# Four split buffers, four open sums in the mix and output products, and a wide value pair in a fused decoder layer on one core

## The chip, the cores and the metric

The kernel runs on one core of one Trainium2 chip. Time is device time in microseconds (us) for one execution of the whole program, the median of several executions.

## What is computed

One decoder layer on 256 tokens of width 1024, in float32, with weights read from HBM. The reference, cut to what matters:

```python
h = x
u = rms_norm(h, norm_mix)
z = u @ w_in                                  # 1024 x 3328
y_rwkv = rwkv7_time_mix(z[:, :1792], ...)     # 8 heads of 64, a recurrence over 256 steps
q, k, v = split(z[:, 1792:], 3)               # 8 heads of 64
y_moba = moba_attention(q, k, v)              # one block of 256: plain causal attention
h = h + concat([y_rwkv, y_moba]) @ w_mix_out
h = h + cross_attention(rms_norm(h, norm_xattn), rms_norm(mem, norm_mem), w_xq, w_xkv, w_xo)  # 4 heads of 256
a = square(relu(rms_norm(h, norm_ffn) @ w_ff1))    # 1024 x 4096
h = h + a @ w_ff2                                  # 4096 x 1024
out = rms_norm(h, norm_final)
```

## The kernel before

**Dense products.** All weights are cut into 65 units of 1 MB (UNITS): z is the part of the input projection for the recurrence, mq and mv the queries, keys and values of the first attention, xk and xv those of the cross-attention's memory, xq its queries, mix and xo the two output products, f1 and f2 the feed-forward part. A unit is loaded by SP into one of three raw buffers and worked off in two halves s. Every half is split for accuracy: ScalarE's hi(s) copies it to w_hi in the rounded type fp32r, VectorE's lo(s) writes the rest, raw - w_hi, to w_lo. TensorE then makes three products for each k: high x high, high x low, low x high. A buffer of w_hi and w_lo is one of NSPLIT = 3, taken in turn, so hi(s) waits for dense_mm, which counts the finished halves, to reach s - 2.

**Quarters.** A half is done in two quarters; QUARTERS lists them as (half, part), 260 in all, and dense(n) in TensorE's program issues the next n. In most units a quarter is 4 of the 8 k steps (12 matmuls of 256 columns). For mix and xo units 0 and 1 the list mixes the quarters of four halves, so that those parts come first whose input is ready first: in mix the attention's part 1, in xo the first two heads' part 0. Sums lie in two banks, dense_bank[0] and [1] (bank 6 and 7), and take(o) on VectorE takes the finished sum o away. A unit is wide (wide_of) if it holds 512 columns of 4 k steps instead of 256 columns of 8; then two units make a pair, the tokens are the stationary side and a matmul is 512 columns long (lines 488 to 490). Only xv 0 and 1 are wide before; mv 0 and 1 use lines 502 to 504, with 256 columns.

**The small work between them.** TensorE's program is a hand-written list in which small steps stand between the calls of dense: mats, right, join and solve (the inverse of the recurrence's blocks), outq, phi, psi, state, states_out (the recurrence over 8 chunks), pair_scores, pair_flip, pair_values (first attention, two heads at a time), scores, turn, values (cross-attention, a head at a time), deviation, normalize, gate (end of the recurrent part). ScalarE and VectorE have lists of their own with the same names, in which hi, lo and take stand between the small steps. blocks() is VectorE's step that inverts 16 x 16 blocks by rank-one updates, one after another; join(0, .) needs its first result, join(1, .) its second and a copy by ScalarE. For head h of the cross-attention scores(h) goes to VectorE (scale, maximum), ScalarE (exponential), VectorE (weigh), TensorE (turn, a transpose), ScalarE (copy), TensorE (values), and then two copies split the result for xo. Every engine works strictly in the order of its list and waits at semaphores.

Of the kernel before, what the change touches and what calls it, by code (L numbers as in the profile page):

```python
# [18 lines left out]
NRAW, NSPLIT = 3, 3  # L19
# [12 lines left out]
def units():  # L32
# [5 lines left out]
    out += [("mv", "w_in", 0, base + 2 * RW + 256 * j, j) for j in range(2)]  # L38
# [18 lines left out]
def wide_of(u):  # L57

    what, _, _, _, j = UNITS[u]
    return  what == "xv" and j < 2  # L60
# [56 lines left out]
def build(nc, io, out):  # L117
# [3 lines left out]
    with ctx:  # L121
# [6 lines left out]
        def flat(x):  # L128
            return x.rearrange("p a t -> p (a t)")
# [30 lines left out]
        btok = sb("btok", [128, NT, RW])  # L160
# [154 lines left out]
        def half_bank(s):  # L315
            return dense_bank[(s + 1) % 2]

# [128 lines left out]
        def _(pe):  # L446
# [4 lines left out]
            def quarter(q):  # L451
# [73 lines left out]
                dst = b[:, (s % 2) * T:(s % 2) * T + T]  # L525
# [434 lines left out]
            spread(0)  # L960
            dense(8)
            lora()
            spread(1)
            dense(4)
            key_sums()
            load(1, 0)
            dense(3)
            keys(0)
            load(1, 1)
            dense(15)  # L970
            tokens()
            dense(2)
            bonus()
            dense(1)
            vtokens()
            dense(3)
# [4 lines left out]
            dense(2)  # L981
            mats(1, 0)
            mats(1, 1)
            load(1, 2)
            mats(1, 2)
            mats(1, 3)
            dense(3)
            right(0)
            right(1)
            dense(2)  # L990
            load(1, 3)
            dense(1)
            join(0, 0)
            join(0, 1)
            join(1, 0)
            dense(2)
            join(1, 1)
            dense(2)
            pair_scores(0)
            solve(0)  # L1000
# [3 lines left out]
            dense(2)  # L1004
            outq(0, 0)
            pair_flip(0)
            dense(2)
            pair_values(0)
            outq(0, 1)
            outq(0, 2)  # L1010
            pair_scores(1)
            outq(0, 3)
            dense(5)
            pair_flip(1)
            outq(1, 0)
# [3 lines left out]
            dense(3)  # L1019
# [3 lines left out]
            dense(3)  # L1023
            pair_scores(2)
            psi(0, 0)
# [7 lines left out]
            dense(3)  # L1033
            state(1)
            pair_flip(2)
            state(2)
            dense(1)
            pair_values(2)
            state(3)
            dense(1)  # L1040
            state(4)
            dense(1)
            state(5)
            pair_scores(3)
            state(6)
            dense(1)
# [4 lines left out]
            dense(1)  # L1051
            normalize()
            dense(3)
            pair_values(3)
            gate()
            dense(20)
# [6 lines left out]
            dense(3)  # L1063
# [6 lines left out]
            dense(1)  # L1070
# [4 lines left out]
            turn(3)  # L1075
            values(3)
            dense(40)
            rms(3)
            dense(47)
            residual(0)  # L1080
            dense(2)
            residual(1)
            dense(34)
            residual(2)
            dense(14)
            residual(3)
            dense(6)
# [3 lines left out]
        def _(act):  # L1091
# [24 lines left out]
            def follow(o):  # L1116
                what, j = OUTS[o][3:5]
                if what == "z":

                    act.wait_ge(dve_params, 2)  # L1120
                    act.wait_ge(out_taken, o + 1)
                    for a in range(2):
                        t = 2 * j + a
                        last = op(zT[:, t, :], tmp[:, 0, a * T:a * T + T], ACT.Copy, scale=onemu[:, t:t + 1])
                    last.then_inc(act_rest, 1)
# [15 lines left out]
            def part(n, half):  # L1141
# [5 lines left out]
                op(tmp[:, n % 2, T * half:T * half + T], half_bank(s)[:, T:2 * T], ACT.Copy).then_inc(act_part, 1)  # L1147
# [204 lines left out]
            hi(3)  # L1352
            follow(0)
            hi(4)
            stats(1)
            hi(5)
            follow(1)
            hi(6)
            gates()
            hi(7)  # L1360
            hi(8)
            follow(2)
            rates()
            key_sums()
            hi(9)
            key_norm()
            follow(3)
            hi(10)
            hi(11)
            decays()  # L1370
            hi(12)
            follow(4)
            hi(13)
            factor()
            load(1, 0)
            hi(14)
            hi(15)
            load(1, 1)
            follow(5)
            hi(16)  # L1380
            follow(6)
            hi(17)
            hi(18)
            tokens()
            hi(19)
            vtokens()
            hi(20)
            hi(21)
            hi(22)
            hi(23)  # L1390
            right(0)
            right(1)
            hi(24)
            load(1, 2)
            join()
            hi(25)
            hi(26)
            right(2)
            load(1, 3)
            right(3)  # L1400
            solve(0)
            hi(27)
            pair_scores(0)
            hi(28)
            solve(1)
            hi(29)
            pair_flip(0)
            pair_values(0)
            hi(30)
            pair_scores(1)  # L1410
            hi(31)
            outq(0)
            hi(32)
            hi(33)
            pair_flip(1)
            outq(1)
            pair_values(1)
            hi(34)
            pair_scores(2)
            hi(35)  # L1420
            source_out(0)
            source_out(1)
            source_out(2)
            hi(36)
            pair_flip(2)
            pair_values(2)
            source_out(3)
            hi(37)
            pair_scores(3)
            hi(38)  # L1430
            deviation()
            hi(39)
            deviation_root()
            pair_flip(3)
            hi(40)
            hi(41)
            hi(42)
            pair_values(3)
            gate(0)
            gate(1)  # L1440
            hi(43)
# [5 lines left out]
            hi(49)  # L1447
            operand("mix", 0)
            operand("mix", 1)
            operand("mix", 2)  # L1450
            hi(50)
            operand("mix", 3)
            hi(51)
            hi(52)
            rms(2)
            hi(53)
            hi(54)
            scores(0)
            hi(55)
            turn(0)  # L1460
            hi(56)
            hi(57)
            scores(1)
            values(0)
            hi(58)
            turn(1)
            scores(2)
            hi(59)
            values(1)
            hi(60)  # L1470
            turn(2)
# [920 lines left out]
```

## Time and profile before

| | |
|---|---|
| median of 3 executions | 467.77 us (467.44 to 468.75) |
| the profiled execution | 468.22 us, span 465.9 us |
| matmuls (PE) busy | 453.1 us, 4488 instructions |
| VectorE (DVE) busy | 320.4 us |
| ScalarE (ACT) busy | 233.8 us |
| granted TensorE clock, mean | 0.997 of 2.4 GHz |

The span runs from the first to the last instruction. Of TensorE's busy time one should know that matmuls overlap in the profile: one is drawn from its start to a modelled end, and the next starts long before that end. What a matmul costs the engine is the distance from its start to the next one's. In the trace's rows a time in brackets is the engine's idle time just before an instruction, with the engine and line that ended it.

### The profile page before, as it was taken

The page shows a single profiled execution, that of the slowest core. Times are in us where ns is not written, and L with a number is a line of the kernel's source. Part 1 is how long each engine was busy: PE and PEld are TensorE (multiplying, and loading weights), DVE is VectorE, ACT ScalarE, POOL GpSimd, SP SyncE. Part 2 cuts the span into 40 slices and gives each one's busy share as a digit, 9 for nine tenths or more (in the row PEclk, how much of TensorE's full clock was granted, in tenths as well). Part 3 has the DMA queues.
Part 4 walks back from the last instruction along what each step waited for, and adds up shares of the span by engine and source line. Part 5 has one row for each costly group of instructions (what it writes and reads, how often), then busy time and mean ns, then how long its engine had stood idle before and what let it go on. Part 6 is the DMA issues. An engine that isn't in the chain of part 4 may idle for free.

```text
span 465.9 us, 10518 instructions
## 1 busy us (share of the span) xinstructions
PE 453.1 (97%) x4488; PEld 410.9 (88%) x4488; DVE 320.4 (69%) x487; ACT 233.8 (50%) x373; POOL 35.1 (8%) x51
## 2 busy tenths in 40 slices
PE   7999999899999999999998999999999999999994
PEld 7999999889998789999997998888888888888883
DVE  4878997887667579579665476846575648555675
ACT  5897843044442544436544355545453544455444
POOL 8200000000000000062000001250000000000000
PEclk9999999999999999999999999999999999999998
DMA  8955544602343223554343256565656474865502
GB/s 258 344 165 174 171 133 138 184 4 94 117 164 112 91 93 110 162 182 166 113 140 126 78 156 218 179 192 174 188 186 204 145 250 141 281 183 184 181 0 90
DMA packets 60385, 73.05 MB, mean 157 GB/s; under 512 B 1314, under 2 KB 49524, under 8 KB 60340
## 3 DMA queue, kind: packets, MB, share of 16 engines
q1 hardware_dynamic: 60260, 72.14, 48.3%
q8 instruction: 35, 0.57, 0.5%
q0 software_dynamic: 80, 0.26, 0.2%
q14 instruction: 10, 0.08, 0.1%
HBM read 71.35 MB, written 1.05 MB: 155 GB/s over the span
## 4 chain that ended last, share of the span: by engine, by line
PE 95%; ACT 2%; DVE 1%; issue 1%; DMA 1%; SPq 0%
PE bank L534 13%; PE bank L549 11%; PE bank L550 11%; PE bank L551 11%; PE bank L568 6%; PE bank L566 6%; PE bank L567 6%; PE bank L536 6%; PE bank L502 2%; PE bank L503 2%; PE bank L504 2%; PE bank L946 2%; PE bank L922 2%; PE bank L488 1%; PE bank L616 1%; PE bank L533 1%
## 5 line engine op out<-in xcount | busy, mean ns | idle before, releaser
L1622 DVE TENSOR_TENSOR w_lo<-raw,w_hi 128x1024 fp32r<-128x1024 f32 x130 | 159.7, 1237 | 55.8 <-ACT w_hi L1114 55.4
L1114 ACT ACTIVATE w_hi<-raw 128x1024 fp32r<-128x1024 f32 x130 | 136.9, 1057 | 101.8 <-PE bank L568 41.7
L534 PE MATMUL bank<-op,w_hi 128*128 128x512 f32 x256 | 89.7, 399 | 0.0
L549 PE MATMUL bank<-op,w_hi 128*128 128x256 f32 x288 | 83.5, 290 | 0.7 <-DVE w_lo L1622 0.7
L551 PE MATMUL bank<-op,w_lo 128*128 128x256 f32 x288 | 81.5, 283 | 0.0
L550 PE MATMUL bank<-op,w_hi 128*128 128x256 f32 x288 | 81.4, 283 | 0.0
L536 PE MATMUL bank<-op,w_lo 128*128 128x256 f32 x224 | 62.9, 281 | 0.0
L549 PEld LDWEIGHTS bank<-op,w_hi 128*128 128x128 f32 x288 | 55.2, 192 | 1.5 <-ACT w_hi L1114 0.8
L550 PEld LDWEIGHTS bank<-op,w_hi 128*128 128x128 f32 x288 | 55.2, 192 | 0.2
L551 PEld LDWEIGHTS bank<-op,w_lo 128*128 128x128 f32 x288 | 55.2, 192 | 0.0
L534 PEld LDWEIGHTS bank<-op,w_hi 128*128 128x128 f32 x256 | 46.6, 188 | 8.9
L566 PE MATMUL bank<-w_hi,op_hi 128*128 128x512 f32 x128 | 50.0, 390 | 0.0
L568 PE MATMUL bank<-w_hi,op_lo 128*128 128x512 f32 x128 | 49.8, 389 | 0.0
L567 PE MATMUL bank<-w_lo,op_hi 128*128 128x512 f32 x128 | 49.8, 389 | 0.0
L536 PEld LDWEIGHTS bank<-op,w_lo 128*128 128x128 f32 x224 | 42.3, 189 | 1.2
L549 PE MATMUL bank<-op_hi,w_hi 128*128 128x256 f32 x128 | 37.2, 290 | 0.0
L550 PE MATMUL bank<-op_lo,w_hi 128*128 128x256 f32 x128 | 36.2, 283 | 0.0
L551 PE MATMUL bank<-op_hi,w_lo 128*128 128x256 f32 x128 | 36.2, 283 | 0.0
L1702 DVE TENSOR_TENSOR tmp<-bank,tmp 128x256 f32<-128x256 f32 x32 | 13.3, 421 | 24.7 <-ACT tmp L1147 24.4
L567 PEld LDWEIGHTS bank<-w_lo,op_hi 128*128 128x128 f32 x128 | 24.0, 188 | 5.0
L568 PEld LDWEIGHTS bank<-w_hi,op_lo 128*128 128x128 f32 x128 | 24.0, 188 | 5.0
L566 PEld LDWEIGHTS bank<-w_hi,op_hi 128*128 128x128 f32 x128 | 24.0, 188 | 4.7
(277 smaller groups left out, 713.4 us busy)
## 6 DMA issues: line engine op xcount, KB each, us to landing
raw<-in_w_ff SPq DMA_DIRECT2D x32, 1024.0 KB, 5.3
raw<-in_w_in SPq DMA_DIRECT2D x12, 1024.0 KB, 6.1
raw<-in_w_xkv SPq DMA_DIRECT2D x8, 1024.0 KB, 5.4
raw<-in_w_mix_out SPq DMA_DIRECT2D x4, 1024.0 KB, 5.1
raw<-in_w_xq SPq DMA_DIRECT2D x4, 1024.0 KB, 5.8
raw<-in_w_xo SPq DMA_DIRECT2D x4, 1024.0 KB, 5.1
xval<-in_x SPq DMA_DIRECT2D x2, 512.0 KB, 4.9
raw<-in_w_in SPq DMA_DIRECT2D x2, 512.0 KB, 5.8
```

Source lines behind the costliest of these rows:

```text
L502: mm(dst, hi, wh[:, k, :], start=(xk == 0), stop=False)
L534: last = mm(b[:, :], wh[:, k, :], op_both[0][:, :, k, :], start=first, stop=final)
L536: mm(b[:, 0:T], wl[:, k, :], op_hi[0][:, k, :], start=False, stop=False)
L549: mm(dst, wh[:, k, :], op_hi[which][:, k, :], start=first, stop=False)
L550: mm(dst, wh[:, k, :], op_lo[which][:, k, :], start=False, stop=False)
L551: last = mm(dst, wl[:, k, :], op_hi[which][:, k, :], start=False, stop=final)
L566: mm(dst[:, :], hi, wh[:, k, :], start=first, stop=False)
L567: mm(dst[:, :], hi, wl[:, k, :], start=False, stop=False)
L568: last = mm(dst[:, :], lo, wh[:, k, :], start=False, stop=final)
L1114: op(view(w_hi), r, ACT.Copy).then_inc(hi_done, 1)
L1622: tt(view(w_lo), r, view(w_hi).bitcast(f32), ALU.subtract).then_inc(lo_done, 1)
L1702: tt(x, half_bank(s)[:, 0:T], x, ALU.add).then_inc(dve_add, 1)
```

## The change

- NSPLIT goes from 3 to 4: a fourth buffer of w_hi and w_lo.
- Room for it: tmp keeps one buffer of its own, its second is the first half of mval, free by then; btok moves into xval.
- mv 0 and 1 become a wide pair: 4 k steps of 512 columns each, with the loads (4 x 512 instead of 8 x 256), the matmuls and the takes of a pair.
- In mix and xo units 0 and 1 the second halves' sums get columns 0 to 255 of bank 1 and bank 2 (second_bank). So four sums can be open, and QUARTERS takes all four early parts first, then the four late ones. TensorE waits for dve_norm before the first such half of mix, and take adds the two halves with two operations.
- The lists of TensorE, ScalarE and VectorE are reordered throughout.

```diff
-NRAW, NSPLIT = 3, 3
+NRAW, NSPLIT = 3, 4
...
-    out += [("mv", "w_in", 0, base + 2 * RW + 256 * j, j) for j in range(2)]
+    out += [("mv", "w_in", 4 * j, base + 2 * RW, j) for j in range(2)]
...
-    return  what == "xv" and j < 2
+    return what == "mv" or what == "xv" and j < 2
...
         QUARTERS += [(2 * _u + _i, _late ^ _p ^ 1) for _i, _p in
-                     ((0, 0), (2, 0), (0, 1), (1, 0), (1, 1), (2, 1), (3, 0), (3, 1))]
+                     ((0, 0), (1, 0), (2, 0), (3, 0), (0, 1), (1, 1), (2, 1), (3, 1))]
...
-        tmp = sb("tmp", [128, 2, 512])
+        tmp = [sb("tmp", [128, 512])[:, :], mval[:, 0, :]]
...
-        btok = sb("btok", [128, NT, RW])
+        btok = flat(xval).rearrange("p (h n c) -> p h n c", h=2, n=NT)[:, 0, :, :]
...
+        def second_bank(o):
+
+            what, j = OUTS[o][3:5]
+            return B[1 + j][:, 0:T] if what in ("mix", "xo") and j < 2 else dense_bank[o % 2][:, T:2 * T]
...
-                dst = b[:, (s % 2) * T:(s % 2) * T + T]
+                dst = second_bank(o) if s % 2 else b[:, 0:T]
+                if what == "mix" and s % 2 and q == BEGUN[s]:
+                    pe.wait_ge(dve_norm, 1)
...
+                    if j < 2:
+                        for a, x in enumerate((dense_bank[o % 2][:, 0:T], second_bank(o))):
+                            last = tt(h[:, a, :], x, h[:, a, :], ALU.add)
+                        last.then_inc(out_taken, 1)
+                        return
...
             join(0, 0)
             join(0, 1)
+            load(1, 2)
+            load(1, 3)
+            dense(6)
             join(1, 0)
-            dense(2)
             join(1, 1)
-            dense(2)
             pair_scores(0)
```

TensorE at the first join, where neu,X is join(0, 0) and (0, 1), neu alone join(1, 0), and xkey the transposes of load. Before:

```order
L504 MATMUL bank7<-w_hi,op0 128x256
L756 MATMUL bank0<-neu,X 32x32 x64
L756 MATMUL bank1<-neu 32x32 x32
L502 MATMUL bank6<-w_hi,op0 128x256
L503 MATMUL bank6<-w_lo,op0 128x256
```

and of the change:

```order
L495 MATMUL bank7<-w_hi,op0 128x512
L763 MATMUL bank0<-neu,X 32x32 x64
L623 MATMUL bank4<-ident,xkey 128x128 x4
L623 MATMUL bank5<-ident,xkey 128x128 x4
L493 MATMUL bank6<-w_hi,op0 128x512
```

The two loads now stand behind join(0, .), and join(1, .) follows six quarters later. The list ahead of it, from mats(1, 3) on, is dense(4), right(0), right(1), dense(1) now, and was dense(3), right(0), right(1), dense(2), load(1, 3), dense(1).

VectorE at the end of blocks(), whose last instruction is the transpose. Before:

```order
L1894 STREAM_TRANSPOSE neu<-neu 128x16x2x16
L1622 TENSOR_TENSOR w_lo<-raw,w_hi 128x1024
L1676 TENSOR_TENSOR mqk<-bank6,rinv 128x512
L1622 TENSOR_TENSOR w_lo<-raw,w_hi 128x1024
L1740 SCALAR_TENSOR_TENSOR op1_lo<-bank4,par,op1_hi 128x256 x2
```

and of the change:

```order
L1903 STREAM_TRANSPOSE neu<-neu 128x16x2x16
L1685 TENSOR_TENSOR mqk<-bank6,rinv 128x512
L1626 TENSOR_TENSOR w_lo<-raw,w_hi 128x1024 x4
L1926 TENSOR_SCALAR s2<-s2,par 128x256 x4
L1749 SCALAR_TENSOR_TENSOR op1_lo<-bank4,par,op1_hi 128x256 x2
```

take(10), the row that writes mqk, comes directly behind blocks(); the splits of four halves follow it in one run, and bonus_bias (s2) has moved here.

TensorE at the end of the cross-attention, where probT,xval is values and ident,prob is turn. Before, values(2), turn(3) and values(3) with nothing between:

```order
L551 MATMUL bank7<-op1_hi,w_lo 128x256
L946 MATMUL bank4<-probT,xval 128x256 x4
L934 MATMUL bank5<-ident,prob 128x128 x4
L946 MATMUL bank4<-probT,xval 128x256 x4
L549 MATMUL bank6<-op1_hi,w_hi 128x256
```

and of the change:

```order
L558 MATMUL bank1<-op1_hi,w_lo 128x256
L953 MATMUL bank4<-probT,xval 128x256 x4
L941 MATMUL bank5<-ident,prob 128x128 x4
L556 MATMUL bank6<-op1_hi,w_hi 128x256
L557 MATMUL bank6<-op1_lo,w_hi 128x256
...
L558 MATMUL bank6<-op1_hi,w_lo 128x256
L953 MATMUL bank4<-probT,xval 128x256 x4
L556 MATMUL bank2<-op1_hi,w_hi 128x256
```

A quarter of xo stands between turn(3) and values(3); the sums in bank 1 and bank 2 are the second halves.

## Rows read from the trace of the kernel before

**Rows 1.** The page's first part: matmuls, busy us, share, instructions.
```profile
PE 453.1 (97%) x4488; PEld 410.9 (88%) x4488; DVE 320.4 (69%) x487; ACT 233.8 (50%) x373; POOL 35.1 (8%) x51
```

**Rows 2.** The page's costliest groups: line, engine, operation | busy, mean ns | idle before, releaser.
```profile
L1114 ACT ACTIVATE w_hi<-raw 128x1024 fp32r<-128x1024 f32 x130 | 136.9, 1057 | 101.8 <-PE bank L568 41.7
```

**Rows 3.** The waits of TensorE: line <- awaited: us in total, times, longest.
```profile
PE bank L737 <- issue: 1.3, 1, 1.3
PE bank L946 <- DVE op_lo L2020: 1.0, 1, 1.0
PE bank L756 <- ACT neu L1254: 0.8, 1, 0.8
PE bank L549 <- DVE w_lo L1622: 0.7, 1, 0.7
```

**Rows 4.** TensorE in order of time (start, length), dense, small, dense again.
```profile
116.11 0.28 PE L549 MATMUL bank<-op_hi,w_hi 128*128 128x256 f32 x1
...
118.14 0.28 PE L551 MATMUL bank<-op_hi,w_lo 128*128 128x256 f32 x1
118.35 0.34 PE L798 MATMUL bank<-X,zT 32*64 32x32 f32 x16
...
119.64 0.36 PE L549 MATMUL bank<-op_hi,w_hi 128*128 128x256 f32 x1
119.84 0.28 PE L550 MATMUL bank<-op_lo,w_hi 128*128 128x256 f32 x1
```

**Rows 5.** The same view, first and last of 48 matmuls of the down projection.
```profile
302.27 0.40 PE L566 MATMUL bank<-w_hi,op_hi 128*128 128x512 f32 x1
...
312.93 0.39 PE L568 MATMUL bank<-w_hi,op_lo 128*128 128x512 f32 x1
```

**Rows 6.** The same view from the last mats to the first join.
```profile
87.69 0.74 PE L737 MATMUL bank<-AR,s 64*32 64x64 f32 x50 [1.33 <-issue]
88.36 0.38 PE L549 MATMUL bank<-op,w_hi 128*128 128x256 f32 x1
...
99.18 0.60 PE L616 MATMUL bank<-ident,xkey 128*128 128x128 f32 x4
...
101.15 1.03 PE L756 MATMUL bank<-neu,X 32*32 32x32 f32 x93
```

**Rows 7.** VectorE in order of time: blocks(), its first row and its two results.
```profile
90.19 1.12 DVE L1878 STREAM_TRANSPOSE neu<-neu 128x512 f32<-128x512 f32 x1
...
99.39 1.14 DVE L1890 STREAM_TRANSPOSE neu<-neu 128x512 f32<-128x512 f32 x1
...
100.94 1.08 DVE L1894 STREAM_TRANSPOSE neu<-neu 128x512 f32<-128x512 f32 x1
```

**Rows 8.** TensorE in the cross-attention: turn L934, scores L922, values L946, dense L549.
```profile
230.40 0.60 PE L934 MATMUL bank<-ident,prob 128*128 128x128 f32 x4
...
232.38 0.47 PE L549 MATMUL bank<-op,w_hi 128*128 128x256 f32 x1
...
236.88 1.89 PE L946 MATMUL bank<-probT,xval 128*128 128x256 f32 x8
238.42 0.47 PE L549 MATMUL bank<-op,w_hi 128*128 128x256 f32 x1
...
248.23 0.60 PE L934 MATMUL bank<-ident,prob 128*128 128x128 f32 x4
...
250.82 0.47 PE L549 MATMUL bank<-op_hi,w_hi 128*128 128x256 f32 x1
...
257.91 0.47 PE L549 MATMUL bank<-op_hi,w_hi 128*128 128x256 f32 x1
```

**Rows 9.** VectorE for the last head: scale, maximum, weigh.
```profile
251.21 0.69 DVE L2006 TENSOR_SCALAR prob<-bank 128x512 f32<-128x512 f32 x1 [0.96 <-PE bank L922]
251.94 0.69 DVE L2007 TENSOR_REDUCE small<-prob 128x2 f32<-128x512 f32 x1
...
253.98 0.62 DVE L2014 TENSOR_SCALAR prob<-prob,small 128x256 f32<-128x256 f32 x2
```

More of the change, by code:

```diff
@@ L960, in _ @@
             spread(0)
+            dense(6)
+            lora()
             dense(8)
-            lora()
+            key_sums()
             spread(1)
-            dense(4)
-            key_sums()
+            dense(2)
+            keys(0)
+            dense(14)
             load(1, 0)
[L967 to L970, printed above, removed]
             tokens()
@@ L973, in _ @@
             bonus()
+            vtokens()
             dense(1)
-            vtokens()
-            dense(3)
             mats(0, 0)
@@ L1003, in _ @@
             solve(3)
-            dense(2)
+            dense(3)
             outq(0, 0)
+            outq(0, 1)
+            outq(0, 2)
             pair_flip(0)
@@ L1018, in _ @@
             outq(1, 3)
-            dense(3)
+            dense(2)
             pair_values(1)
@@ L1023, in _ @@
             dense(3)
+            psi(0, 0)
             pair_scores(2)
-            psi(0, 0)
+            dense(2)
             psi(0, 1)
@@ L1032, in _ @@
             psi(1, 3)
-            dense(3)
+            dense(1)
             state(1)
+            dense(2)
+            state(2)
             pair_flip(2)
-            state(2)
+            state(3)
             dense(1)
             pair_values(2)
-            state(3)
-            dense(1)
             state(4)
@@ L1043, in _ @@
             state(5)
+            dense(1)
+            state(6)
             pair_scores(3)
-            state(6)
-            dense(1)
             states_out()
@@ L1062, in _ @@
             scores(1)
-            dense(3)
+            dense(2)
             values(0)
@@ L1069, in _ @@
             values(1)
-            dense(1)
+            dense(2)
             turn(2)
@@ L1499, in _ @@
             hi(74)
+            part(2, 0)
+            hi(75)
             part(2, 1)
+            part(3, 0)
             follow(34)
-            hi(75)
             hi(76)
-            part(3, 0)
             hi(77)
+            follow(35)
             part(3, 1)
@@ L1682, in shift @@
                     t = 2 * j + a
-                    last = stt(out=zT[:, t, 1:T], in0=tmp[:, 0, a * T:a * T + T - 1], scalar=gain("rwkv_mu", t),
+                    last = stt(out=zT[:, t, 1:T], in0=tmp[0][:, a * T:a * T + T - 1], scalar=gain("rwkv_mu", t),
                                in1=zT[:, t, 1:T], op0=ALU.mult, op1=ALU.add)
@@ L1700, in add @@
                 dve.wait_ge(act_part, 2 * n + half + 1)
-                x = tmp[:, n % 2, T * half:T * half + T]
+                x = tmp[n % 2][:, T * half:T * half + T]
                 tt(x, half_bank(s)[:, 0:T], x, ALU.add).then_inc(dve_add, 1)
@@ L2049, in _ @@
             load(0, 1)
-            copies(0)
             load(0, 2)
@@ L2054, in _ @@
             params(1)
+            copies(0)
             diagonal_of(0)
@@ L2059, in _ @@
             lo(3)
+            lo(4)
+            sides()
             follow(0)
-            lo(4)
+            lo(5)
+            take(1)
             copies(1)
-            take(1)
-            lo(5)
-            lo(6)
             diagonal_of(1)
             follow(1)
+            lo(6)
+            lo(7)
+            lo(8)
             take(2)
             follow(2)
-            lo(7)
-            lo(8)
+            lo(9)
+            sums()
+            take(3)
+            lo(10)
+            lo(11)
+            key_norm()
+            follow(3)
             spread_copy(1)
-            sums()
-            key_norm()
-            take(3)
             key_root()
-            lo(9)
-            lo(10)
-            follow(3)
-            lo(11)
+            lo(12)
+            take(4)
             keys(0)
-            take(4)
             keys(1)
-            lo(12)
+            lo(13)
             follow(4)
-            lo(13)
             take(5)
+            lo(14)
             keys(2)
-            lo(14)
-            keys(3)
             lo(15)
@@ L2214, in _ @@
             values(0)
-            lo(57)
+            scores(2)
             lo(58)
-            scores(2)
+            lo(59)
             weigh(2)
```

406 lines of the change are left out of this document (200 added, 206 removed).

## The prediction, made before the changed kernel was run

> **What bounds the kernel now.** The page's first part comes first: matmuls occupy TensorE for 97% of a 465.9 us span [rows 1]. The profiled execution took 468.22 us, 2.3 us more than its span; the median of the three runs is 467.77 us, so a sum made against the profile is lowered by 0.45 us at the end. A busy share can hide small gaps, because a 256-column matmul is drawn 0.28 us long while the next one starts after 0.12 us [rows 4]. So I read starts, not lengths. In the long stretches the starts are evenly spaced, and the list of TensorE's waits holds only a few microseconds [rows 3]. TensorE sets the time, and there are only three ways to shorten it: fewer columns or cheaper instructions on it, fewer changes between dense and small work, and the few waits. Idle time of the other engines is worth nothing by itself. The copies that split the weights (w_hi, ScalarE) follow 101.8 us of idling, mostly for TensorE itself [rows 2]: they are early. No wait in the list is for a buffer that has not been freed. A fourth split buffer alone therefore brings nothing; it only permits the new orders.
>
> **The attention's value units as a wide pair.** Before, they are 96 matmuls of 256 columns: two units, two halves, two parts, four k, three products. The start of one follows that of the last by 0.119 us: 17 steps from 116.11 to 118.14 [rows 4]. After, they are 48 of 512 columns. The down projection has the same form, and there 47 steps take from 302.27 to 312.93, 0.227 us each [rows 5]. 96 x 0.1194 = 11.46 us become 48 x 0.2268 = 10.89 us, a gain of **0.57 us**, all on TensorE's path. At least nothing is lost (the columns are the same), so 0 to 0.6.
> The trace shows 0.119 and 0.227 us, so each instruction carries some 12 ns beside its columns. The Trainium skill (TensorE: Matmul & The Clock Gate, Back-to-back issue gap) gives an isolated gap of N/2.4 + 2.5 ns; as an estimate from that page the pair would gain only 0.1 us. The same section gives 131 ns as the sustained spacing at 512 columns, by which it would gain 5 us; the rows speak against both.
>
> **Fewer changes of work.** A small block between dense quarters costs extra at both ends: 118.14 to 118.35 going out, 119.64 to 119.84 coming in [rows 4], each 0.08 to 0.09 us above the step, 0.17 us together. The order has 41 separate dense stretches before and 38 after: 3 x 0.17 = **0.5 us** (0 to 0.6).
>
> **The end of the cross-attention.** From turn(2) at 248.23 to the dense stretch at 257.91 pass 9.68 us [rows 8]. The work in it, by the undisturbed rows of the same group: turn with scores 1.98 (230.40 to 232.38), a quarter with its changes 12 x 0.119 + 0.17 = 1.60, values 1.54 (236.88 to 238.42) twice, turn 1.98 - 1.54 = 0.44; together 7.10. So 2.58 us are waits, of which the list names 1.0 for op_lo [rows 3]; most of the rest hides in drawn lengths. The cause is that turn(3) and values(3) stand directly behind values(2), while VectorE and ScalarE still make the softmax. After, xo's second halves have banks of their own, so two quarters more can be opened: xo's first quarter moves ahead of turn(2), which lets take(28) be ready for scores(3), one quarter stands between turn(3) and values(3), another behind values(3). Counted from turn(2) = 0: scores(3) ends at 1.98, the quarter at 3.58. VectorE's scaling starts 0.4 after the scores end (250.82 [rows 8] to 251.21) and with the maximum ends 1.42 later, at 252.63 [rows 9]; so values(2) can start at 3.87, a wait of 0.3. Exponential and weighing take from 252.63 to 254.60 [rows 9], 1.97, so turn(3) starts at 5.85 against 5.41, a wait of 0.45. Values(3) comes 1.6 us after turn(3)'s end, and what it needs is two copies of 0.6: no wait. 2.58 becomes 0.75: **1.8 us** gained. If a copy or split that stands between them on ScalarE or VectorE is late, 1 us less; if the order hides all, 2.6.
>
> **The wait of join(1, 0).** Before, it follows join(0, 1) at once and waits 0.8 us for ScalarE's copy [rows 3]. After, two loads and six quarters lie between. **0.8 us** go.
>
> **What is late instead.** The inverse's blocks() are a chain on VectorE. The last mats ends at 88.36 [rows 6]; blocks() begins at 90.19, its first result is there at 99.39 + 1.14 = 100.53, 12.2 us after the mats, and its second at 102.02, 13.7 us after [rows 7]. Before, TensorE came to join(0, 0) at 101.15, 12.8 us after the mats [rows 6], in time, having done six quarters, both right() and a load. After, it has five quarters, one of them wide, and no load: 12.8 - 1.43 - 0.5 (the load with its change) - 0.07 = 10.8 us. It waits 1.4 us. Just behind it the second part of the wide unit needs the bank that take(10) frees, and take(10) is queued behind all of blocks(): 13.7 + 0.6 + 0.1 = 14.4. TensorE, after that wait, arrives there at 12.2 + 1.4 (two join; 93 of their 128 instructions are drawn 1.03 us long [rows 6]) + 0.7 (two loads) = 14.3. So the two waits fall together, **1.5 us lost** in all. Queued behind them on VectorE is lo(23), ready at 15.5, wanted at 15.9. If VectorE is 0.4 us later, that adds; if blocks() starts earlier, at most 0.5 is won back: loss 1.0 to 2.3.
>
> **The issue gap in mats.** TensorE stood 1.33 us in mats(1, 2), waiting for no other engine [rows 3, 6]. It had then issued some 230 matmuls since mats(0, 0) in 6 us. After, the same count is reached about 1 us later, but mats(1, 0) to (1, 3) stand in one piece. The trace of before cannot tell whether it stays whole (0) or goes (1.33). I take the middle, **0.7 us**.
>
> **At no cost, with the cover named.** The first wait, 0.7 us for w_lo [rows 3], stays, since the split that ends it keeps its place behind ScalarE's squares of x, which the change does not touch. take of mix and xo 0 and 1 becomes two VectorE operations of 256 columns, about 0.1 us more each: the next user of the bank comes two quarters (2.9 us) later. mix's four open sums give the gate chain four quarters of cover instead of two: the two quarters more, 2.9 us, cover what the earlier place of gate() takes away. btok inside xval and tmp inside mval need no new wait of TensorE: xval is next written by take(17), behind state(6). The Pool sums and all weight DMAs keep their order; the value pair's two DMAs carry the same megabyte each in longer rows. The DMA of unit u still waits for both splits of unit u - 3, which come no later.
>
> **Sum.** 0.57 + 0.5 + 1.8 + 0.8 - 1.5 + 0.7 = 2.9 us. 468.2 - 2.9 = 465.3 for an execution like the profiled one, 464.9 against the median; I say **465.0 us**.
>
> **Rivals.**
> *The waits only move.* In a fixed order each engine stands where its next instruction stands. If the cross-attention keeps 1.5 us more than I count, because of a split queued ahead of the softmax, and the issue gap stays (0.7), 2.2 of the 2.9 are gone: 467.0. For it: my walk leaves values(2) and turn(3) with no slack at all. Against: both waits are short there, and the covers added are whole quarters.
> *More is won.* The issue gap goes (0.6 beyond the sum) and VectorE reaches blocks() 0.5 earlier: 463.9.
> *Slower: ScalarE and VectorE stand in line for the fourth buffer.* With four buffers a split may run further ahead and is placed so, but its turn comes before the half that frees it is done, and what stands behind it is held. The place: source_out(2) behind hi(38), the state steps behind both; then lo(43) ahead of gate_lo, and in the feed-forward part() behind hi(). Its price is up to one quarter, 1.43 us, each time. It decides once four such places fall on the path: 5.7 - 2.9 gives 470.6. Against: the idling before w_hi is 101.8 us over 130 copies, so a held copy has room, and the state steps keep a dense quarter between most of them.
> *The change does nothing for the path* except the columns: 467.2, if new waits eat the rest; it joins the first rival.
>
> **How the numbers follow.** A measurement of this kernel can tell about 0.3%, 1.4 us, from no change. The forecast with its unknowns (464.2 to 466.3) has 0.50; more is won 0.18; the waits only move (466.4 to 467.9) 0.23; slower by the queue 0.09. Faster by over 0.3% (under 466.4) is 0.50 + 0.18 + a little of the moved waits = 0.70, within 0.3% 0.22, slower 0.08. The ends of my unknown costs are: pair 0 to 0.6, changes 0 to 0.6, cross-attention 0.8 to 2.6, late blocks -2.3 to -1.0, issue gap 0 to 1.33. The range 463.4 to 467.3 leaves out the tails where several of them fall on the same side.
>
> **What would show it.** In the profile after: 48 matmuls of 128x512 in the value units, 0.227 us apart; no wait of join(1, 0) but one of 1.3 to 1.5 us at join(0, 0), for VectorE's blocks; from turn(2) to the dense stretch behind values(3) about 1.8 us less waiting; the issue wait absent or smaller; the feed-forward stretch unchanged in its steps. I am wrong if TensorE waits in the state steps, ahead of gate_lo, or in the feed-forward part, or if join(0, 0) does not wait.

## The result, and the profile after

The changed kernel takes **474.27 us** (median of 5 runs, 473.71 to 474.55); the kernel before, run beside it, 467.91 us (5 runs, 467.44 to 468.79). The ratio is 1.0133, 95% interval 1.0119 to 1.0146: slower by 1.3%, where 465.0 us (463.4 to 467.3) was predicted. The profiled execution has a span of 472.2 us against 465.9.

The page's first part, to set beside [rows 1], shows that hardly anything was added to any engine's work:
```profile
PE 452.8 (96%) x4440; PEld 407.8 (86%) x4440; DVE 320.4 (68%) x489; ACT 234.0 (50%) x373; POOL 35.5 (8%) x51
```
48 matmuls are gone, as planned. (The splits' idle time is 98.4 us against the 101.8 of [rows 2].) The loss must be idle time or a lower clock of TensorE. Its waits (line <- awaited: us in total, times, longest), to set beside [rows 3]:
```profile
PE bank L744 <- issue: 2.2, 1, 2.2
PE bank L558 <- issue: 2.2, 1, 2.2
PE bank L763 <- DVE neu L1899: 1.5, 1, 1.5
PE bank L763 <- issue: 1.3, 1, 1.3
PE bank L623 <- DMA xval<-in_x: 1.1, 1, 1.1
PE bank L606 <- DMA prob<-in_rwkv_ln_b: 1.0, 1, 1.0
PE bank L556 <- DVE op L1702: 0.9, 1, 0.9
```
The reader should see three things. Where [rows 3] had one "issue" of 1.3 us, there are three, together 5.7. There is one wait for blocks() (L763, neu), 1.5, and no wait for ScalarE's neu. And there is a wait of 0.9 for an operand (L1702) that nobody had foreseen. "issue" means that the engine waited for nothing that the profile shows, for no semaphore and no transfer of the kernel. In order of time (start, length), TensorE around the three:
```profile
82.25 0.27 PE L558 MATMUL bank<-op,w_lo 128*128 128x256 f32 x1 [2.18 <-issue]
...
84.96 1.30 PE L744 MATMUL bank<-AR,s 64*32 64x64 f32 x106
88.45 0.36 PE L744 MATMUL bank<-AR,s 64*32 64x64 f32 x19 [2.18 <-issue]
...
111.79 1.18 PE L763 MATMUL bank<-neu 32*32 32x32 f32 x89
114.25 0.26 PE L763 MATMUL bank<-neu 32*32 32x32 f32 x6 [1.28 <-issue]
114.44 1.03 PE L894 MATMUL bank<-mqk 64*128 64x128 f32 x8
...
115.99 0.63 PE L494 MATMUL bank<-w_lo,op 128*128 128x512 f32 x1
116.42 0.63 PE L495 MATMUL bank<-w_hi,op 128*128 128x512 f32 x1
```
The first gap is in the middle of a dense quarter, the second within mats(1, *), the third within join(1, *), six matmuls before the end of join(1, 1). Behind the third the wide matmuls stand 0.43 us apart; seven us earlier, undisturbed, the same ones stood 0.23 apart, the spacing of [rows 5]:
```profile
108.70 0.39 PE L493 MATMUL bank<-w_hi,op 128*128 128x512 f32 x1
108.93 0.39 PE L494 MATMUL bank<-w_lo,op 128*128 128x512 f32 x1
```
Busy time by stretch (start:end, us, PE busy and instructions, granted clock, DMA share, GB/s) shows that TensorE ran at the lower of its two levels, 1.2 GHz, for 3.4 us from 115.1 on.
```profile
114.00:116.00 2.00, 1.75 (x16) 0.78 0.84 237
116.00:118.00 2.00, 2.00 (x6) 0.50 0.87 296
118.00:120.00 2.00, 2.00 (x61) 0.86 0.00 0
```

**What stands in the DMA queues at that time.** The page's third part lists, beside the kernel's own transfers (q1), a queue of instruction transfers:
```profile
q8 instruction: 35, 0.57, 0.5%
```
35 packets of 16 KB for 4440 matmuls and as many weight loads: one for about 127 matmuls. The gaps fit that: with the program's first matmul counted as 0, they stand ahead of matmuls 718, 846 and 1352, which are 128 and 506 (4 x 126.5) apart, and the gap of the kernel before stands ahead of 846 too. In the second trace of the changed kernel and in its variants below (the runs named a_, a_narrow aside), every gap of over 0.2 us stands ahead of 718, 846, 1352, 1478 or 2366, again whole packets apart. So a gap opens where one packet's matmuls end and the next one's should begin.

The same list for short stretches of the changed kernel says when they run. From 76 to 79.8 us, from 79.8 to 81, from 81 to 85.9, and from 85.9 to 87.2 (packets, MB, share of 16 engines' time; where transfers overlap a share can exceed 100%):
```profile
q1 hardware_dynamic: 460, 0.94, 76.3%
...
q1 hardware_dynamic: 61, 0.09, 21.6%
q8 instruction: 1, 0.02, 4.9%
...
q1 hardware_dynamic: 970, 1.00, 68.9%
...
q1 hardware_dynamic: 77, 0.06, 16.0%
q8 instruction: 1, 0.02, 5.2%
```
While unit 12's megabyte moves there is no instruction packet; one comes as it ends. The same with unit 13. TensorE resumes 1.3 to 1.4 us after the end of each such packet: 80.82 to 82.25, 87.06 to 88.45, and in join 112.99 to 114.25, again just behind a pair of loads (105.1 to 111.9 us). In the kernel before, the first of the two instruction packets slipped in as the load began, and only the second came late; from 77.7 to 79, from 79 to 85.2 and from 85.2 to 86.5 us:
```profile
q1 hardware_dynamic: 228, 0.23, 76.8%
q8 instruction: 1, 0.02, 5.6%
...
q1 hardware_dynamic: 1842, 1.86, 92.1%
...
q8 instruction: 1, 0.02, 5.4%
```
That second packet ends at 86.4, and TensorE's gap of [rows 6] ends at 87.69. So **theory 1**: a packet of TensorE's instructions stands behind weight loads that are on their way, and the new orders bring unit 12's load further forward (SyncE issues it at 75.71, before at 76.62), so that the packet which used to slip in now stands behind it, and two more loads onto the packet of join(1, *). **Theory 2**, the rival: the new order puts mats(1, 0) to (1, 3) and all of join(1, *) in one piece, 128 small matmuls in 1.4 us, and these outrun the fetch whatever else moves. A third reading, that unit 12's rows of 2 KB (1 KB before) hold the packet up, is answered by b_wide below: with the same rows in the old order there is no first gap, and the second is 0.6 us (1.3 in b_fourwide).
The Trainium skill (Runtime: NRT & Kernel Launch, Instruction fetch mechanics) says that instructions arrive in 16 KiB blocks of 256, through a DMA queue of the sequencer's own, and that this is mostly hidden. The size agrees with the row (2 x 127 in a packet). "Hidden" does not: 5.7 us of gaps here.

### The profile page after: what moved, and what is told of

Its sections match the earlier page's. It is cut to its first block, busy times and chain, and to the rows that moved or that the text cites. A ratio compares the mean times of both kernels' runs of the same rounds, so it can differ in the third digit from the quotient of the medians.

```text
span 472.2 us, 10423 instructions
## 1 busy us (share of the span) xinstructions
PE 452.8 (96%) x4440; PEld 407.8 (86%) x4440; DVE 320.4 (68%) x489; ACT 234.0 (50%) x373; POOL 35.5 (8%) x51
## 4 chain that ended last, share of the span: by engine, by line
PE 89%; DVE 4%; issue 2%; DMA 2%; SPq 1%; ACT 1%; ACTq 0%
PE bank L541 13%; PE bank L556 10%; PE bank L558 10%; PE bank L557 10%; PE bank L574 6%; PE bank L573 6%; PE bank L575 6%; PE bank L543 6%; PE bank L493 2%; PE bank L494 2%; PE bank L495 2%; DMA raw<-in_w_in 2%; PE bank L953 2%; PE bank L929 1%; DVE op L1702 1%
## 5 line engine op out<-in xcount | busy, mean ns | idle before, releaser
L1118 ACT ACTIVATE w_hi<-raw 128x1024 fp32r<-128x1024 f32 x130 | 135.7, 1057 | 98.4 <-PE bank L558 36.6
L558 PE MATMUL bank<-op,w_lo 128*128 128x256 f32 x288 | 81.5, 283 | 2.2 <-issue 2.2
L556 PEld LDWEIGHTS bank<-op_hi,w_hi 128*128 128x128 f32 x128 | 24.5, 191 | 1.0 <-issue 0.9
```

What stands on the lines that cost most here:

```text
L556: mm(dst, wh[:, k, :], op_hi[which][:, k, :], start=first, stop=False)
L558: last = mm(dst, wl[:, k, :], op_hi[which][:, k, :], start=False, stop=final)
L1118: op(view(w_hi), r, ACT.Copy).then_inc(hi_done, 1)
```

## The experiments

Times are medians in us; the ratio is to the kernel before, run beside it (its medians were 467.9 to 468.4). Between runs made at different times the ratios compare better than the us. The gaps are those of the one kept trace.

| run | what | time | ratio, 95% | gaps of TensorE ("issue"), us |
|---|---|---|---|---|
| a_again | changed, unchanged | 475.05 | one run | 2.2, 2.5, 0.7, 0.5, 1.2 |
| b_again | before, unchanged | 468.75 | one run | 1.1 |
| a_hold | units 12, 13, 14, 15 held | 468.31 | 1.0005 [0.9992, 1.0019] | 1.1 |
| b_hold | before, 12 to 14 held | 469.42 | 1.0029 [1.0010, 1.0047] | 1.2, elsewhere |
| a_hold1 | unit 12 held a little | 472.81 | one run | 0.9, 1.3, 1.4 |
| a_spread | mats spread again | 473.75 | one run | 1.4, 1.0 |
| b_wide | before, wide pair alone | 484.26 | 1.0370 [1.0337, 1.0403] | 0.6, 3.4, 1.8 |
| b_fourwide | and fourth buffer | 484.50 | 1.0374 [1.0343, 1.0405] | 1.3, 3.8, 1.5 |
| a_fix | holds, operand in front | 466.21 | 0.9968 [0.9956, 0.9980] | 0.2 |
| a_tail | a_fix, old end | 467.69 | 0.9986 [0.9974, 0.9999] | none |
| a_fix2 | better holds | **464.53** | 0.9913 [0.9897, 0.9929] | none |
| a_best | loads ahead of join | 465.08 | 0.9925 [0.9909, 0.9940] | 0.3, 0.2 |
| a_free | a_fix2, 12 and 13 let go | 468.98 | 1.0018 [0.9996, 1.0040] | 1.6, 0.8 |
| b_hold2 | before, better holds | 467.19 | 0.9982 [0.9963, 1.0001] | 0.5 |
| a_narrow | a_fix2, narrow pair | 469.82 | 1.0030 [1.0012, 1.0047] | 0.4, 1.9 |

**Do the gaps repeat?** Both kernels once more.

> The kernel before once more, unchanged, for a second trace. Both theories take its one issue gap (1.33 us in mats(1, 2), matmul 846 of TensorE's stream) as a property of the order: it should stand at the same place with the same length within 0.2 us, at a span of 465.9 us within 0.6. If it is gone or elsewhere, gaps of a single trace prove nothing and both theories need more traces.

> The changed kernel once more, unchanged, for a second trace. Both theories expect the three issue gaps (2.18 us at 80.1 and 2.18 us at 86.3 between dense work and mats, 1.28 us in join(1, 0) at 113.0) and the half clock from 115 to 118.5 us again, each within 0.3 us. The wait of 1.0 us for the parameters' transfer at the start may be chance: then it differs here and the span is 471.2 instead of 472.2.

The gap of before repeats in its place, ahead of matmul 846 (1.1 us). Of the changed kernel the two gaps at mats repeat (2.18 and 2.46 us, at 81.7 and 88.2); the third splits into 0.7 in join(1, 1) and 0.5 in the solve, and a new one of 1.2 appears in psi. The wait for the parameters at the start is gone here: it is chance. The low clock comes elsewhere, at 87.7 us and for 6.8 us, where the largest gap is. So the two gaps at mats belong to the order; the later ones vary in length, and where the clock falls varies.

**Holding the loads.** SyncE issues a weight load as soon as both splits have freed its buffer. Here it also waits until the small work is done:
```
-                w = io[src].rearrange("l (k p) n -> p (l k) n", p=128)
+                if u in (12, 13):
+                    sp.wait_ge(pe_mats, 2)
+                if u in (14, 15):
+                    sp.wait_ge(pe_join, 2)
+                w = io[src].rearrange("l (k p) n -> p (l k) n", p=128)
```


> The changed kernel, with SyncE holding two pairs of weight loads: units 12 and 13 until the last mats is done, units 14 and 15 until the last join is done. Theory 1: TensorE's instruction fetches stand behind the megabyte loads that run at the same time; with no load on its way during mats and join, the gaps of 2.2, 2.2 and 1.3 us go, and if the half clock was brought on by the last of them, 1.4 us more: 474.3 - 5.7 - 1.4 = 467 us (467 to 469.5). Theory 2: 128 small matmuls in 1.4 us outrun the fetch whatever else runs: gaps and time stay (473.5 to 474.5), or the time rises where a held load comes late.

468.31 us: 6.0 us came back, and the clock does not fall before the last 2 us. The two packets that start at 79.9 and 86.0 us in the changed kernel start at 76.9 and 80.7 here. TensorE's order, and with it the dense packing of the small matmuls, is untouched, so theory 2 falls: packing alone makes no gap. It can still be what makes a late packet cost so much. Its two longest waits now, the start aside:
```profile
PE bank L767 <- DVE neu L1903: 1.5, 1, 1.5
PE bank L851 <- issue: 1.1, 1, 1.1
```
(Lines are 4 higher.) The gap in psi, L851, is the one that a_again also had: its packet starts at 151.3 us, where unit 20's load (148.1 to 151.5) is all but through.

The same on the kernel before, with 12, 13 and 14 held until the last mats:

> The kernel before, with SyncE holding units 12, 13 and 14 until the last mats is done. Theory 1: its gap of 1.33 us in mats(1, 2) goes, 466.5 us, unless the held loads delay a split by more. Theory 2: the gap stays, 467.8 us.

The gap in mats went, as expected, and the time did not: a gap of 1.2 us appeared in join, at 102.73, ahead of matmul 1227, three packets behind 846. The median even rose by 1.5 us, clear of no change; the kept trace, of a 468.23 us run, does not show why. The three loads now move in one piece from 89.0 to 99.8 us, and no packet passes from 89 to 95; one follows from 95 to 97, and the next only between 99.8 and 101.3:
```profile
q1 hardware_dynamic: 1904, 1.93, 101.2%
...
q1 hardware_dynamic: 690, 0.69, 109.0%
q8 instruction: 1, 0.02, 3.5%
...
q8 instruction: 1, 0.02, 3.9%
```
That is the strongest sign for theory 1: in a kernel whose TensorE order did not change, **the gap followed the loads**. With unit 14 waiting for the last join instead (b_hold2), most of it goes:

> The kernel before, units 12 and 13 held until the last mats and unit 14 until the last join. With unit 14 behind the other two the gap had moved from mats to join (1.2 us). Theory: now neither has one: 468.0 - 1.3 = 466.7 us, ratio 0.997. If the held unit 14 makes ScalarE late at hi(28) as in the changed kernel, 1 to 1.5 us are lost at outq: 468.

467.19, 1.0 us less than before and 2.2 less than b_hold, with 0.5 us of a gap left; the interval just touches no change.

**How much earlier is too early?** Unit 12 alone, held by some 2 us, until mats(0, 3) is done (`sp.wait_ge(pe_mats, 1)` for `u == 12`).

> The changed kernel with unit 12 alone held until mats(0, 3) is done, some 2 us later than now. Theory 1 (fetches stand behind the loads): the fetch that starts at 76.9 us when the way is free now comes before the load, so the first gap of 2.18 us goes; the load then covers the two fetches that mats(1, *) needs, so a gap of 1.3 to 3.5 us stays there; span 470 to 472. Theory 2 (small matmuls outrun the fetch): both gaps stay as they were, span 472 to 473.

As theory 1 has it: the first gap is gone, the second is 0.86 us, less than expected; 1.3 in join and 1.4 in psi (the place of a_again's) are there, and behind each of these two the clock is at 1.2 GHz for 3.4 us. The span is 470.7.

**Spreading the small work again**, all loads as they are.
```
             mats(0, 3)
-            load(1, 1)
-            dense(3)
+            dense(2)
             mats(1, 0)
             mats(1, 1)
+            load(1, 1)
+            dense(2)
             mats(1, 2)
             mats(1, 3)
-            dense(4)
+            dense(3)
```


> The changed kernel with all loads as they are, but TensorE's dense quarters again between the mats as before: two behind mats(0, 3), two more and load(1, 1) behind mats(1, 1), three behind mats(1, 3). Theory 1 (a fetch that stands behind the two loads): the first gap, which falls into dense work, stays near 2.2 us, since it hangs on the fetch that ends at 80.9; the second may shrink by up to 0.7, as TensorE asks for the next instructions later. Rival (the bunching is the cause): both gaps shrink to the 1.3 us of the kernel before in all.

This one tells little: it was not the clean test that it was meant to be. Moving load(1, 1) made ScalarE, whose order was not changed, stand for it:
```profile
83.41 0.84 ACT L1171 ACTIVATE op_hi<-bank,par 128x256 fp32r<-128x256 f32 x2 [7.75 <-PE bank L623]
```
The splits behind it were late, and so was unit 13's load (87.6 instead of about 83 us), which freed the second packet; join(0, 0) then waited 4.7 us. Of the first two gaps one is left, the first, at 1.4 us where theory 1 expected 2.2; another of 1.0 stands in psi, the clock is low for 6.8 us within and behind the wait at join, and the time is 473.75. A placement rule for the small work can't be read from it.

**The parts alone, in the old order.** The wide pair, and the wide pair with the fourth buffer:
```
-    out += [("mv", "w_in", 0, base + 2 * RW + 256 * j, j) for j in range(2)]
+    out += [("mv", "w_in", 4 * j, base + 2 * RW, j) for j in range(2)]
...
-    return  what == "xv" and j < 2
+    return what == "mv" or what == "xv" and j < 2
```


> The kernel before with the attention's value units as a pair of 512 columns and nothing else. The sum of the prediction: 0.57 us less on TensorE, 467.4, ratio 0.9988; the issue gap and all waits as before. Rival: the wide first half holds its bank longer and take comes late, a new wait of up to 1.4 us at the next unit, 468.8.

> The kernel before with the wide pair and the fourth split buffer (and the two tiles moved for its room), all orders and the open sums as before. The prediction's claim that the buffer alone brings nothing: the same as with the wide pair alone, 467.4, within 0.4. Theory 1's side effect: splits that run further ahead let SyncE issue its loads earlier, so the issue gap may move or grow by up to 1 us: then 468.4.

**16.4 and 16.6 us slower.** A wide half takes a whole bank, so its first quarter needs take(10) to be done, and take(10) stands behind blocks() on VectorE. TensorE, then VectorE:
```profile
95.74 0.66 PE L774 MATMUL bank<-ident,AR 128*128 128x128 f32 x4
103.88 0.80 PE L488 MATMUL bank<-w_hi,op 128*128 128x512 f32 x1 [7.48 <-DVE mqk L1676]
...
101.13 1.04 DVE L1894 STREAM_TRANSPOSE neu<-neu 128x512 f32<-128x512 f32 x1
...
103.15 0.68 DVE L1676 TENSOR_TENSOR mqk<-bank,rinv 128x512 f32<-128x512 f32 x1
```
To this come gaps of 3.4 and 1.8 us and 10.2 us at 1.2 GHz, 6.8 of them from within this wait on. So the 0.57 us of the pair was not to be had in the old order. The fourth buffer added 0.2 us, no difference beside runs that spread over 4.6 us: it brings nothing there. The buffer without the pair was not run.

**The rest of the losses.** Four holds (12 and 13 until the last mats, 14 until the last join, 20 until `pe_psi`), and on VectorE:
```
             operand("mix", 2)
+            operand("mix", 3)
             lo(51)
             take(24)
-            operand("mix", 3)
```


> The changed kernel with units 12 and 13 held until the last mats, 14 until the last join, 20 until the last psi, and VectorE's operand(mix, 3) ahead of lo(51) and take(24). The kernel with the first three holds took 468.3 us with a gap of 1.1 us in psi (its fetch came at the end of unit 20's load) and 0.9 us of waiting for the operand. Theory 1: both go, 466.3 us (465.8 to 467), ratio to before 0.9965. Theory 2: the gap in psi stays, 467.4 us.

466.21, as expected, and faster than before. Its kept trace is of its slowest run, 468.53 us, with 3.4 us at 1.2 GHz from 123.0 us on. A wait of 1.6 us at outq(0, 0), L805, just ahead of that, showed what a hold can cost. ScalarE:
```profile
115.54 1.06 ACT L1118 ACTIVATE w_hi<-raw 128x1024 fp32r<-128x1024 f32 x1 [2.72 <-DMA raw<-in_w_xkv]
116.50 0.58 ACT L1262 ACTIVATE U<-bank 128x512 f32<-128x512 f32 x1
```
It stands for the held unit 14 with a copy of the solve behind it. So unit 14 is let go, 15 held in its place, and VectorE's solve(3) put back ahead of pair_weigh(0):

> The kernel with four holds, unit 14 let go and unit 15 held instead until the last join, and VectorE's solve(3) ahead of pair_weigh(0). With unit 14 held, ScalarE stood 2.7 us in hi(28) ahead of a copy of solve, and TensorE 1.55 us at outq(0, 0) for VectorE's copy behind the softmax weights. Theory 1: the load of unit 14 ends before the fetch for join(1, *) is asked for, so no gap comes back, and the wait at outq goes: 466.2 - 1.5 = 464.7 us (464.3 to 465.6). Otherwise the gap of up to 1.3 us comes back in join(1, 0): 466.

**464.53 us**, 0.9913 of before, 9.7 less than the changed kernel; no gap at all, no fall of the clock before the last us. Its queue from 76 to 79.8, 79.8 to 81.5 and 81.5 to 85.2 us:
```profile
q8 instruction: 1, 0.02, 1.5%
...
q8 instruction: 1, 0.02, 3.6%
...
q8 instruction: 1, 0.02, 1.6%
```
Three packets pass freely in a stretch where the changed kernel had one. Both mats go through without a pause; the second, 128 in 1.5 us:
```profile
82.13 1.49 PE L744 MATMUL bank<-AR,s 64*32 64x64 f32 x128
```
**Undoing one hold in it**, that of 12 and 13:

> The kernel without any issue gap (464.5 us) with one thing undone: units 12 and 13 are no longer held until the last mats. If the fetches behind these two loads are the cause, the two gaps of 2.2 us in the dense stretch ahead of mats(1, *) and in mats(1, *) come back: 464.5 + 4.4 = 468.9 us, and up to 470.5 if TensorE's clock falls behind them as in two traces of the changed kernel. If the clock and the gaps had the other holds or orders as their cause, the time stays within 1 us of 464.5.

468.98: 4.4 us came back, as much as the two gaps of the changed kernel together. The gaps of that median run were not seen: the kept trace is of the fastest run, 466.98 us, and its gaps of 1.6 and 0.8 account for its 2.4 us over a_fix2. The runs go from 466.98 to 472.92 us, while those of a_fix2 lie between 464.25 and 465.13. It fits that with loads in the way a packet's lateness, or the clock, varies from run to run, but only one run has a trace.

**One step more**, load(1, 2) and load(1, 3) ahead of join(0, 0), and take(10) between blocks()' two results:

> The kernel before this one in the list, with load(1, 2) and load(1, 3) ahead of join(0, 0), and VectorE's take(10) between the first and the second result of blocks(). Join(0, 0) still waits for the first result; the dense quarter behind it no longer needs the loads and take(10) in between: 0.8 us less, 463.9 us if a_fix2 comes to 464.7. Rival: the issue fetches shift with it and a new gap eats it, the same time as a_fix2.

No gain: 465.08, 0.5 us more than a_fix2. The wait at join(0, 0) shrinks from 1.5 to 0.6, but that is the loads' time; the dense quarters behind it start 0.9 earlier, lose 0.6 of it again, most of that waiting for lo(23), which is still behind blocks(), and a gap of 0.3 in join(1, 1) takes the rest. The rival was right.

**The end of the cross-attention** in the old order, in a_fix:
```
-            dense(2)
+            dense(1)
             turn(2)
...
             turn(3)
-            dense(1)
             values(3)
-            dense(58)
+            dense(60)
```


> The kernel with four holds and the operand in front (466.2 us), with TensorE's order at the end of the cross-attention as before: one quarter ahead of turn(2) instead of two, values(3) directly behind turn(3). The prediction gives 1.8 us for that order: 468.0 (467.0 if only TensorE's place counts and the changed orders of VectorE and ScalarE carry the rest).

467.69 against 466.21: **1.5 us** for the order. The two were not run side by side, and by their ratios to the kernel before it is 0.8. The traces, which no startup or clock disturbs behind values(1), give 1.9: from the start of values(1) to the last matmul 214.36 us in a_tail (245.63 to 459.99) and 212.48 in a_fix (247.59 to 460.07). So 1.8 stands within what can be told, and the wait of 1.0 us for op_lo of [rows 3] is back (L953 <- DVE op_lo).

**The wide pair undone** in a_fix2, all orders as they are:

> The kernel without any issue gap (464.5 us) with the attention's value units as two of 256 columns again, all orders as they are. By the sum of the prediction 0.57 us more on TensorE: 465.1. Rival: TensorE's waits at join(0, 0) absorb part, since a narrow quarter order frees a bank earlier: 464.5 to 464.9; and the other side, more instructions to fetch between mats and join bring a gap back, 466.

469.82, 5.3 us more, ten times the term. In its profile, span 466.6 against 462.5, a gap of 1.9 us at 156.8 and one of 0.4 at 122.7 account for 2.3, the low clock from 96.8 to 100.2 for most of the rest. The two gaps stand ahead of matmuls 1732 and 2494, where no other trace has one: 48 matmuls more shift every later packet against the loads. That the holds, placed for the other stream, no longer fit is likely and was not tested. The 0.57 us can't be told apart from that.

## Why the prediction was wrong

**The step that failed** is "The issue gap in mats": "it stays whole (0) or goes (1.33)", 0.7 us taken. The bound was too narrow on one side. The gap was treated as something that the order of TensorE has or has not; it could also grow, and it did, from 1.33 to 5.64 us. The term should have read -4.3, not +0.7. The sentences that hid it stand further down: all weight DMAs "keep their order", and the splits that free their buffers "come no later". They came no later; unit 12's load came 0.9 us *earlier*. That the place of the loads was the harm is shown by a_hold, a_hold1 and a_free; how much of the growth comes from the earlier load and how much from mats(1, *) standing in one piece is not, since a_spread was not clean. The trace of before had what was needed: a packet of the instruction queue at 77.8 us and none until 85.2, and the gap's end 1.3 us behind the second.

**What came with it** and had no term: the granted clock. From pair_scores(0) to solve(0), one wide quarter, the changed kernel takes 3.82 us (114.44 to 118.26) and a_fix2 2.46 (107.70 to 110.16): 1.4 us.

**Whose turn it is on VectorE**: operand(mix, 3) now stands behind lo(51) and take(24). The cross-attention's first xq unit waits for it:
```profile
223.19 1.21 DVE L1626 TENSOR_TENSOR w_lo<-raw,w_hi 128x1024 fp32r<-128x1024 f32 x1
224.32 0.86 DVE L1669 TENSOR_SCALAR xval<-bank,row_sum 128x256 f32<-128x256 f32 x2
225.11 0.86 DVE L1702 SCALAR_TENSOR_TENSOR op<-hT,par,op 128x256 fp32r<-128x256 f32 x2
```
0.95 us lost. The order of the change showed it; the prediction followed takes and splits there, not operands.

**How it adds up.** The ladder, changed kernel against a_fix2, from the starts of the same instruction in both traces: first mats 0.5 us later, right(0) 5.3, pair_scores(0) 6.7, solve(0) 8.1, state(1) 8.5, scores(0) 9.7, last matmul 9.7. Two gaps, the third, the clock and the operand are the steps of it. Against the kernel before, whose span is 6.3 us shorter: 4.3 more in gaps, 1.4 of the clock, 0.95 for the operand and 1.8 more in the waits at the start (4.8 against 3.0 us; they lie anywhere from 2.9 to 4.9 in the traces of both orders, so this is chance), less the 2.2 that the other terms of the prediction should gain.

**What was right.**
- The columns. Wide matmuls stand 0.23 us apart, and 48 are fewer. The 0.57 us that this should gain, and the 0.5 for fewer changes of work, no run shows by themselves.
- The late blocks: a wait of 1.4 us at join(0, 0) was predicted, 1.5 lost with what follows; the wait is 1.51. The last mats ends at 88.8, blocks()' first result is there at 100.9 (12.2 us after the mats was predicted), to set beside [rows 6, 7]:
```profile
99.85 1.04 DVE L1899 STREAM_TRANSPOSE neu<-neu 128x512 f32<-128x512 f32 x1
...
100.94 0.74 PE L763 MATMUL bank<-neu,X 32*32 32x32 f32 x63 [1.51 <-DVE neu L1899]
```
- The end of the cross-attention, to set beside [rows 8]; predicted were values(2) 3.87 and turn(3) 5.85 us behind turn(2), with waits of 0.3 and 0.45:
```profile
257.91 0.60 PE L941 MATMUL bank<-ident,prob 128*128 128x128 f32 x4
...
261.80 1.97 PE L953 MATMUL bank<-probT,xval 128*128 128x256 f32 x8
263.73 0.65 PE L941 MATMUL bank<-ident,prob 128*128 128x128 f32 x4
265.65 1.89 PE L953 MATMUL bank<-probT,xval 128*128 128x256 f32 x8
```
3.89 and 5.82. The term, 1.8, measured 1.5 by the medians and 1.9 in the traces (a_tail).
- The wait of join(1, 0) for ScalarE is gone, 0.8 us. The fourth buffer added nothing to the wide pair in the old order, and the rival of the queue for it did not come: no wait in the state steps, ahead of gate_lo or in the feed-forward part.
- The sum. With the gap wholly gone it says 2.9 + 0.6 = 3.5 us. Between the spans of the kernel before and of a_fix2, where gap, clock and operand are mended (and VectorE's solve(3) stands earlier), lie 3.4 us, between their medians 3.9 (468.40 and 464.53). That the first figure comes so close is partly luck: a_fix2's waits at the start are 0.9 us longer. The prediction described a kernel that is nearly the one of 464.53 us; what was run was that kernel with 9.7 us of stalls on top.

**What stays open.** That a gap is TensorE short of its next packet is shown by the places of the gaps; that the packet stands behind the loads is inferred from its start times and from how the gaps follow the loads. When TensorE asks for it is in no row. Nor is it clear when the clock falls: behind a gap of 1.3 it did and behind one of 2.2 it did not, in the same trace; a wait of 1.5 at join(0, 0) was followed by a fall in a_narrow and not in a_fix2.

## What to carry to other kernels

Where a program issues small matmuls as quickly as here (128 in 1.4 us), TensorE's own instructions are a transfer with a due time: put the instruction queue's packets beside the bulk loads before changing either order, and keep megabyte loads out of the two or three us in which a packet is due. A load can be too early: let it wait for the end of the small work, but not so long that an in-order engine stands for it with something urgent behind. And a term of half a us can't be summed as long as shifting the stream by that much can open a gap of two; let the gap's term range to a multiple of its present length, not only down to nothing.

## What was not expected of the hardware

- One packet of 16 KB for 127 matmuls and their weight loads takes 0.9 to 2.3 us itself, and TensorE resumes 1.3 to 1.4 us behind its end, in the three gaps of the changed kernel and in that of before.
- Such gaps stand at fixed places of the instruction stream, whole packets of about 127 matmuls apart; which of these places shows one depends on the loads.
- The gap can open in dense work too: at 79.9 us TensorE stood when only 14 matmuls of 0.12 us had followed 128 small ones and four transposes.
- After or within a stall of 1.3 us and more TensorE was granted 1.2 GHz for 3.4 or 6.8 us, at different places in two traces of one kernel (115.1 and 87.7 us), and not after every such stall.
- A change worth 0.57 us of columns cost 16.4 us in one order, and its removal 5.3 us in another.
